# Per-layer input product moved into the last pair of the second attention, gate taken token half by token half, squares of two layer norms summed by VectorE

## The chip, the core and the metric

The kernel runs on one core of a Trainium2 chip. The metric is the device time of one execution in microseconds (us); lower is better. TensorE (PE in the profile, PEld for its weight loads) multiplies, ScalarE (ACT) applies functions and copies, VectorE (DVE) adds and scales, GpSimd (POOL) splits weights, and DMA queues are fed by SyncE (SP) and by ScalarE (ACTq). Each engine runs its own list of instructions in order and waits on semaphores for the others.

## What is computed

A hybrid layer (convolution and windowed attention), then a layer with forgetting attention and a feed-forward net, for 1024 tokens of width 1024 in float32. The change touches the end of it. With `x` the output of the first layer:

```python
o = fox_mixer(x, w_in, b_f, w_out)             # second attention: 16 heads, causal, log forget gates
y = layer_norm(ALPHA * x + o, ln_mix_g, ln_mix_b)
f = conv_ffn(y, w_up, conv_w, conv_b, w_down)
y = layer_norm(ALPHA * y + f, ln_ffn_g, ln_ffn_b)
out = y + sigmoid(y @ ple_w_gate + ple_b_gate) * (p @ ple_w_proj)
```

`p` is the per-layer input, 256 features for each token; `p @ ple_w_proj` depends on nothing else in the kernel.

## The kernel before

Activations stand feature-major: a tile has 128 features on the partitions, `KT` = 8 tiles make the width, and the 1024 tokens are the free axis, cut into two halves of 512 (`HALF`, `hs(h)`). Each float32 operand is kept as a high part and a low part, and a product of a weight block and an operand block is three matmuls (hi by hi, hi by lo, lo by hi) of 512 columns. A *unit* is a 128-column slab of a weight matrix: SyncE loads it in two pieces into `raw`, GpSimd's `split` makes `whi` and `wlo` of it, in one of two slots. Half a product tile (8 k-blocks, 24 matmuls) goes to `bank0` or `bank1`; its eviction raises `tile_out`.

**The second attention** runs head pair by head pair (`forget_pair`, 8 pairs). A pair has 16 steps s: 8 query blocks for each of two heads, with 1 to 8 key blocks. In a step, in program order: TensorE transposes the probabilities (`flip_p(s)`), multiplies the values of the step before at even s (`values(s - 1)`), and makes `scores(s + 3)`. ScalarE does `normalise(s + 1)`, the fold of the pair of heads at s = 4, 8, 12 (`fold`), copies the transposed block out (`high(s)`, which at even s also waits for `values(s - 1)`), and does `expo(s + 2)`. VectorE does maximum (`maxima(s + 2)`), low part (`low`) and reciprocal (`inverse(s + 2)`). Between the steps of a pair TensorE computes the input product of the following pair. The last pair has none to compute after its first eight blocks. The attention's output is split by `forget_hi` (ScalarE, 128x1024 into `a_lo`) and `forget_lo` (VectorE, into `a_hi`): tiles 0 to 3 in steps 0, 1, 2 and 9 of the last pair, tiles 4 to 7 behind it.

**The output product** (`out_half`) goes through all tiles for token half 0, then for half 1. VectorE evicts each with two operations, ALPHA times the high and ALPHA times the low part of x, and adds it to `acc` for the mean. During half 1 the layer norm n1 of half 0 runs: TensorE multiplies `acc` by a matrix of 1/1024 (`mean`), VectorE subtracts (`centre`), ScalarE squares (`square`), TensorE sums the squares over features (`squares`, one float32 product for each tile), ScalarE takes ln and exp (`root`), and VectorE and ScalarE scale and split (`scaled_and_lo`, `norm_hi`). `half_pass(0)` of the feed-forward net waits for these.

**The end.** The down products of half 1 (`down_half`) run with the norm n2 of half 0 among them. Behind them stand the eight `ple_tile`s (p times its weight: 16 halves of 12 matmuls), with the mean and the eight `squares` of half 1 between, and then `gate_half` for 8 units and 2 halves; each unit of the gate is split once. Sigmoid, product, sum and store follow tile by tile.

Order is written out by hand in each engine's list; nothing is scheduled automatically.

Of the kernel before, what the change touches and what calls it, by code (L numbers as in the profile page):

```python
# [166 lines left out]

LEAVES = {s + 1: PARTS[s][-1] // 8 for s in range(NST) if PARTS[s][-1] % 8 == 7}
# [5 lines left out]
def build(nc, xT, weights, pair_weights, cols, pT, out, y_scr, ga_scr, t_scr, g_scr, c_scr, h_scr):  # L174
    ctx = ExitStack()
    with ctx:
# [52 lines left out]
        def psum(name, n):  # L229
# [45 lines left out]
            ("f_fold", [P, HALF], F32), ("f_raw", [P, S], F32), ("fk_lo0", [P, S], F32R))  # L275
        f_klo = ((fk_lo0, fk_lo1_even), (fk_lo0, fk_lo1_odd))
# [56 lines left out]
        p_hi = ((slot_hi[12], slot_lo[12]), (slot_hi[21], slot_lo[21]))  # L333
        ple = [slot_f[2 * m:2 * m + 2] for m in range(KT)]
        g_sig, g_out = slot_f[16:18], slot_f[18:20]
        (p_raw,) = overlay(stage_b_at, ("p_raw", [P, PLE_KT, S], F32))
        (p_lo,) = overlay(stage_b_at, ("p_lo", [P, PLE_KT, S], F32R))

# [22 lines left out]
        mg_in = [sem(f"mg_in{s}") for s in range(2)]  # L361
# [6 lines left out]
        c_in = [sem(f"c_in{h}") for h in range(2)]  # L368
        z_part = sem("z_part")
        zeros_made = sem("zeros_made")  # L370
# [24 lines left out]
        cols_made = sem("cols_made")  # L395
        p_in = sem("p_in")
        ple_hi = sem("ple_hi")
        ple_lo = sem("ple_lo")
# [84 lines left out]
        def _(pool):  # L483
# [121 lines left out]
        def _(pe):  # L605
# [172 lines left out]
            def forget_pair(it, pp, fills):  # L778
# [1860 lines left out]
```

## Time and profile before

| | us |
|---|---|
| median of 3 runs (lowest, highest) | 2717.56 (2715.29, 2719.19) |
| the profiled execution | 2716.53 |
| its span in the trace | 2714.6 |
| TensorE busy | 2611.3 (96%) |
| VectorE, ScalarE, GpSimd busy | 1405.0, 1061.5, 1276.3 |

All stretches below are from this one execution, in us from the start of its span. The last pair of the second attention lies at about 1690 to 1766, the output product behind it up to about 1873, the last down product ends at about 2585.6, and the last gate matmul is issued at 2708.97. The clock of TensorE is given as a share of full speed: 1.00 is 2.4 GHz, 0.50 is 1.2 GHz.

### The profile page before, as it was taken

The page shows a single profiled execution, that of the slowest core. Times are in us where ns is not written, and L with a number is a line of the kernel's source. Part 1 is how long each engine was busy: PE and PEld are TensorE (multiplying, and loading weights), DVE is VectorE, ACT ScalarE, POOL GpSimd, SP SyncE. Part 2 cuts the span into 40 slices and gives each one's busy share as a digit, 9 for nine tenths or more (in the row PEclk, how much of TensorE's full clock was granted, in tenths as well). Part 3 has the DMA queues.
Part 4 walks back from the last instruction along what each step waited for, and adds up shares of the span by engine and source line. Part 5 has one row for each costly group of instructions (what it writes and reads, how often), then busy time and mean ns, then how long its engine had stood idle before and what let it go on. Part 6 is the DMA issues. An engine that isn't in the chain of part 4 may idle for free.

```text
span 2714.6 us, 37373 instructions
## 1 busy us (share of the span) xinstructions
PE 2611.3 (96%) x12136; PEld 2103.9 (78%) x12136; DVE 1405.0 (52%) x2033; ACT 1061.5 (39%) x1932; POOL 1276.3 (47%) x1060
## 2 busy tenths in 40 slices
PE   8999999999999989999999999799999999999999
PEld 5788888877777778888888888576778888787777
DVE  5455542035555655435555555556865655613443
ACT  4333321065455531127677766603333333301231
POOL 3788873332222214431111111075688787576733
PEclk9999999999999999999999999799999999999999
DMA  2222225310111114221111111021222222633312
GB/s 102 83 77 67 64 98 177 108 39 32 45 40 39 39 70 140 95 78 38 46 40 39 39 39 40 8 86 62 90 85 81 81 82 71 207 97 124 102 56 83
DMA packets 94718, 202.99 MB, mean 75 GB/s; under 512 B 10384, under 2 KB 10512, under 8 KB 94624
## 3 DMA queue, kind: packets, MB, share of 16 engines
q1 hardware_dynamic: 69824, 127.43, 14.9%
q10 hardware_dynamic: 24800, 74.36, 7.7%
q8 instruction: 52, 0.85, 0.1%
q14 instruction: 42, 0.34, 0.0%
HBM read 169.18 MB, written 32.57 MB: 74 GB/s over the span
## 4 chain that ended last, share of the span: by engine, by line
PE 78%; DVE 9%; ACT 7%; issue 4%; POOL 1%; DMA 1%; ACTq 0%; DVEq 0%; POOLq 0%
PE bank L611 18%; PE bank L669 17%; PE bank L872 13%; PE flip L872 6%; PE flip L1032 4%; PE pv L1032 4%; PE bank L1078 3%; PE pv L872 3%; PE pv L822 2%; PE score L631 1%; DVE z L1884 1%; PE flip L807 1%; PE score L794 1%; PE bank L807 1%; PE score L791 1%
## 5 line engine op out<-in xcount | busy, mean ns | idle before, releaser
L516 POOL TENSOR_SCALAR whi<-raw 128x512 fp32r<-128x512 f32 x334 | 252.9, 757 | 1277.1 <-PE bank L669 724.2
L518 POOL TENSOR_TENSOR wlo<-raw,whi 128x512 fp32r<-128x512 f32 x334 | 478.9, 1434 | 27.8
L611 PE MATMUL bank<-a_hi,whi 128*128 128x512 f32 x464 | 185.4, 400 | 3.5 <-POOL wlo L518 2.0
L611 PE MATMUL bank<-a_lo,whi 128*128 128x512 f32 x464 | 186.2, 401 | 0.5 <-DVE a_hi L2030 0.5
L669 PE MATMUL bank<-b_hi,whi 128*128 128x512 f32 x384 | 154.9, 403 | 5.6 <-DVE fk_lo_odd L2024 3.2
L611 PE MATMUL bank<-b_hi,whi 128*128 128x512 f32 x368 | 148.4, 403 | 9.8 <-DVE b_lo L1894 7.7
L531 POOL TENSOR_TENSOR wlo<-a,whi 128x512 fp32r<-128x512 f32 x102 | 148.5, 1455 | 14.5 <-ACT whi L1401 14.5
L669 PE MATMUL bank<-a_hi,whi 128*128 128x512 f32 x368 | 148.9, 405 | 6.2 <-DVE s_z L1971 5.1
L669 PE MATMUL bank<-b_hi,wlo 128*128 128x512 f32 x384 | 151.7, 395 | 0.0
L669 PE MATMUL bank<-b_lo,whi 128*128 128x512 f32 x384 | 151.3, 394 | 0.0
L611 PE MATMUL bank<-b_lo,whi 128*128 128x512 f32 x368 | 146.7, 399 | 2.3 <-DVE b_hi L1926 2.3
L669 PE MATMUL bank<-a_hi,wlo 128*128 128x512 f32 x368 | 145.5, 395 | 0.0
L669 PE MATMUL bank<-a_lo,whi 128*128 128x512 f32 x368 | 145.4, 395 | 0.0
L611 PE MATMUL bank<-a_hi,wlo 128*128 128x512 f32 x336 | 132.6, 395 | 0.0
L1401 ACT ACTIVATE whi<-a 128x512 fp32r<-128x512 f32 x102 | 63.4, 628 | 123.5 <-PE bank L872 51.5
L1299 ACT ACTIVATE fp<-fp,neg_max 128x128 f32<-128x128 f32 (+7 forms) x128 | 99.2, 775 | 26.9 <-DVE neg_max L2050 26.3
L1305 ACT ACTIVATE fp<-fp,row_inv 128x128 f32<-128x128 f32 (+7 forms) x128 | 99.4, 776 | 25.7 <-DVE row_inv L2055 24.9
L611 PEld LDWEIGHTS bank<-a_hi,whi 128*128 128x128 f32 x464 | 87.7, 189 | 26.2 <-issue 4.4
L611 PEld LDWEIGHTS bank<-a_lo,whi 128*128 128x128 f32 x464 | 87.7, 189 | 25.3 <-issue 2.8
L2046 DVE CUSTOM_DVE_ANT_0 fp<-score,fc 128x128 f32<-128x128 f32 (+7 forms) x128 | 96.6, 755 | 15.2 <-issue 5.4
L611 PE MATMUL bank<-b_hi,wlo 128*128 128x512 f32 x240 | 95.6, 398 | 0.0
L611 PEld LDWEIGHTS bank<-b_hi,whi 128*128 128x128 f32 x368 | 70.0, 190 | 30.2 <-DVE b_lo L1894 10.2
(526 smaller groups left out, 7285.8 us busy)
## 6 DMA issues: line engine op xcount, KB each, us to landing
raw<-in_w SPq DMA_DIRECT2D x334, 256.0 KB, 2.6
a<-in_pairs SPq DMA_DIRECT2D x136, 256.0 KB, 2.6
h_scr<-up_y ACTq DMA_DIRECT2D x22, 512.0 KB, 2.6
fc<-c_scr ACTq DMA_DIRECT2D x16, 512.0 KB, 3.6
stage<-h_scr ACTq DMA_DIRECT2D x22, 256.0 KB, 3.4
a<-h_scr ACTq DMA_DIRECT2D x21, 256.0 KB, 3.6
y_scr<-up_y ACTq DMA_DIRECT2D x8, 512.0 KB, 2.7
t_scr<-y_room ACTq DMA_DIRECT2D x8, 512.0 KB, 3.0
```

The lines of the kernel that those rows point to most:

```text
L516: nc.gpsimd.tensor_scalar(hi, src, 1.0, 1.0, ALU.mult, ALU.mult).then_inc(w_hi, 1)
L518: nc.gpsimd.tensor_tensor(lo, src, hi.bitcast(F32), ALU.subtract).then_inc(w_lo, 1)
L531: nc.gpsimd.tensor_tensor(ring[1][pos], src[:].rearrange("p (k c) -> p k c", c=P), ring[0][pos].bitcast(F32), ALU.subtract).then_inc(ww_lo, 1)
L611: last = nc.tensor.matmul(psum_ap, ws[w][:, k, :], a[:, kt, hs(h)], start=(first and i == 0 and j == 0), stop=(final and i == n - 1 and j ...
L669: last = nc.tensor.matmul(bank[b][:], ws[slot][:, k, :], a[:, k, hs(h)], start=(k == 0 and j == 0), stop=(k == KT - 1 and j == 2))
L872: last = nc.tensor.matmul(dst[:], ring[w][pos][:, k, :], a, start=(k == 0 and j == 0), stop=(k == KH - 1 and j == 2))
L1032: last = nc.tensor.matmul(down_bank[m % 2][:], w[ws][:, wk, :], a, start=(k == 0 and j == 0), stop=(k == FT - 1 and j == 2))
L1078: last = nc.tensor.matmul(bank[h][:], w[u % 2][:, k, :], a, start=(k == 0 and i == 0), stop=(k == KT - 1 and i == 2))
L1299: nc.scalar.activation(fp[s % 3][:, 0:w], fp[s % 3][:, 0:w], ACT.Exp, bias=neg_max[:, one], accum_out=row_sum[:, one]).then_inc(fx.exp, 1)
L1305: nc.scalar.activation(fp[s % 3][:, 0:w], fp[s % 3][:, 0:w], ACT.Copy, scale=row_inv[:, s % 4:s % 4 + 1]).then_inc(fx.prob, 1)
L1401: nc.scalar.activation(ring[0][pos], src[:].rearrange("p (k c) -> p k c", c=P), ACT.Copy).then_inc(ww_hi, 1)
L2046: v.tensor_tensor_reduce(out=fp[s % 3][:, 0:w], in0=score[s % 2][:, 0:w], in1=fc[hh][:, 0:w], scale=SCALE, scalar=-3.0e38, op0=ALU.subtrac ...
```

## The change

- `ple_tile` goes away from the end. In the last pair `ple_part(i)` computes half h = i % 2 of output tile m = i // 2 (6 to a half where `p` is kept whole: 2 k-blocks by 3 matmuls), always in `bank[0]`, at the end of the step that `PLE_LATE` names (part s - 2 in steps 2 to 11), two of them early (`PLE_EARLY`). Even parts are evicted by ScalarE, odd ones by VectorE, at the end of the step that `PLE_OUT` names (part s - 3 in steps 3 to 11), into the last tile of `b_lo`; ScalarE issues a store of each to a scratch tensor `ple_scr`. A part starts when the part before it has been evicted.
- For that room GpSimd first adds the halves of x: `b_hi_f = b_hi + b_lo`, 8 operations of 128x1024 (`x_whole`). The attention output's high part goes to `b_lo` instead of `a_lo`, for tiles 0 to 6 in steps 1 to 7, tile 7 behind the pair. `p` is loaded by two DMAs on ScalarE's queue and split in steps 0 and 1.
- The eviction of the output product loses its second operation (low part of x).
- For n1 of half 0 and n2 of both halves the squares are added by VectorE (`square_add`, 7 of them), and TensorE does one product on the sum (`square_sum`).
- The gate goes through all 8 units for half 0, then again for half 1: 16 units are loaded and split. `mean(n2, 1)` stands behind the first, `square_sum(n2, 1)` behind the second.
- The stored parts are loaded again by 16 DMAs of 256 KB on ScalarE's queue. Product, sum and store of the output are made in place there, one half tile at a time.

```diff
+PLE_EARLY = {12: (10,), 15: (14,)}
+PLE_OUT = {s: (s - 3,) if s < 12 else (9, 10) if s == 12 else (s - 2,) for s in range(3, NST)}
+PLE_LATE = {s: s - 2 if s < 12 else s - 1 if s < 15 else s for s in range(2, NST)}
...
+            for j in range(KT):
+                nc.gpsimd.tensor_tensor(b_hi_f[:, j, :], b_hi[:, j, :].bitcast(F32), b_lo[:, j, :].bitcast(F32), ALU.add).then_inc(x_whole, 1)
...
+            def square_sum(ns, h, adds):
+
+                pe.wait_ge(ns.summed, adds)
+                nc.tensor.matmul(score[1][:, hs(h)], feat_mean[:], acc[:, hs(h)], start=True, stop=True).then_inc(ns.sq_used, KT)
...
+            def ple_part(i):
+
+                m, h = divmod(i, 2)
+                u = U_PLE + m // 4
+                if i == 0:
+                    pe.wait_ge(conv_lo, KT + PLE_KT)
+                if h == 0:
+                    pe.wait_ge(w_lo, u * 2 + 2)
+                    pe.wait_ge(tile_out[0], T_PLE + m)
+                    pe.wait_ge(tile_out[1], T_PLE + m)
+                else:
+                    pe.wait_ge(tile_out[0], T_PLE + m + 1)
+                for k in range(PLE_KT):
+                    for j, (ws, a) in enumerate(((whi, p_hi[k]), (whi, p_lo[k]), (wlo, p_hi[k]))):
+                        last = nc.tensor.matmul(bank[0][:], ws[u % 2][:, 2 * (m % 4) + k, :], a[:, hs(h)],
+                                                start=(k == 0 and j == 0), stop=(k == PLE_KT - 1 and j == 2))
+                last.then_inc(tile_done[h], 1)
...
                     flip_p(s)
                     if s and s % 2 == 0:
                         values(s - 1)
+                    if not fills:
+                        for i in PLE_EARLY.get(s, ()):
+                            ple_part(i)
                     if s + 3 < NST:
                         scores(s + 3)
+                    if not fills and s in PLE_LATE:
+                        ple_part(PLE_LATE[s])
...
-                elif j <= 4:
-                    squares(n1, 0, (2 * j - 2, 2 * j - 1))
+                elif j == 4:
+                    square_sum(n1, 0, KT - 1)
...
+            gate_half(0)
+            mean(n2, 1)
+            gate_half(1)
+            square_sum(n2, 1, 2 * (KT - 1))
+            for i in range(2, 2 * KT):
+                gate_half(i)
...
+            def square_to_sum(ns, h, j):
+
+                act.wait_ge(ns.centred, h * KT + j + 1)
+                if j >= 3:
+                    act.wait_ge(ns.summed, h * (KT - 1) + (j - 2))
+                dst = sq[j % 2][:] if j else acc[:, hs(h)]
+                nc.scalar.activation(dst, z[:, j, hs(h)], ACT.Square).then_inc(ns.sq, 1)
...
             def forget_hi(j):
 
-                act.wait_ge(fx.o, 4 * (NPAIR - 1 if j < 4 else NPAIR))
-                nc.scalar.activation(a_lo[:, j, :], f_o[:, j, :], ACT.Copy).then_inc(fx.o_hi, 1)
+                act.wait_ge(fx.o, 4 * (NPAIR - 1 if j < KT - 1 else NPAIR))
+                act.wait_ge(x_whole, j + 1)
+                if j == KT - 1:
+                    for h in range(2):
+                        act.wait_ge(ple_stored[h], 16 * KT)
+                nc.scalar.activation(b_lo[:, j, :], f_o[:, j, :], ACT.Copy).then_inc(fx.o_hi, 1)
...
+            def ple_out(i):
+
+                m, h = divmod(i, 2)
+                room = b_lo_f[:, KT - 1, hs(h)]
+                if h == 0:
+                    if m:
+                        act.wait_ge(ple_stored[0], 16 * m)
+                    else:
+                        act.wait_ge(x_whole, KT)
+                    act.wait_ge(tile_done[0], T_PLE + m + 1)
+                    nc.scalar.activation(room, bank[0][:], ACT.Copy).then_inc(tile_out[0], 1)
+                act.wait_ge(tile_out[h], T_PLE + m + 1)
+                act.dma_start(ple_scr[m, :, hs(h)], room).then_inc(ple_stored[h], 16)
...
             for j in range(KT):
                 out_half(j, j // 2, j % 2, 1, KT + j)
+                for k in range(max(2 * j - 2, 1), min(2 * j, KT)):
+                    square_add(n1, 0, k)
...
             for j in range(KT):
                 centre(n2, 1, j)
-            scaled_and_lo(n2, 1, None, None, C_LN2G, C_LN2B, range(KT))
+            for j in range(1, KT):
+                square_add(n2, 1, j)
```

TensorE, last pair, around step 4 (`flip`, `bank`: transposed probabilities; `pv`: values; `score`: scores). Before:

```order
L807 MATMUL flip<-ident,fp_121 128x128 x3
L807 MATMUL bank<-ident,fp_121 128x128 [waits fx_lo]
L822 MATMUL pv<-fp_hi,fv 128x256 [waits fx_lo]
...
L791 MATMUL score<-fk_114,fq_113 128x512 [waits fx_max]
L794 MATMUL score<-fk_lo_129,fq_113 128x512
L791 MATMUL score<-fk_114,fq_113 128x512
L793 MATMUL score<-mask_r,ident_r 128x128
L794 MATMUL score<-fk_lo_129,fq_113 128x512
L807 MATMUL flip<-ident,fp_122 128x128 [waits fx_lo,fx_prob]
```

In the changed kernel (`fq_even`, `fk_even`, `p_lo` hold the parts of p here):

```order
L820 MATMUL score<-fk_114,fq_113 128x512
L822 MATMUL score<-mask_r,ident_r 128x128
L823 MATMUL score<-fk_lo_129,fq_113 128x512
L803 MATMUL bank<-fq_even,whi_52 128x512 [waits tile_out1,tile_out0,w_lo]
L803 MATMUL bank<-p_lo_131,whi_52 128x512
L803 MATMUL bank<-fq_even,wlo_54 128x512
L803 MATMUL bank<-fk_even,whi_52 128x512
L803 MATMUL bank<-p_lo_132,whi_52 128x512
L803 MATMUL bank<-fk_even,wlo_54 128x512
L836 MATMUL flip<-ident,fp_122 128x128 [waits fx_lo,fx_prob]
```

A part of six matmuls, with its wait on both `tile_out`, now stands between the scores and the transposes of the next step.

ScalarE, last pair, steps 3 and 4. Before:

```order
L1313 ACTIVATE fp_hi<-bank 128x4x128 [waits fx_flipped]
L1299 ACTIVATE fp_122,row_sum<-fp_122,neg_max 128x768 [waits fx_neg_max]
L1305 ACTIVATE fp_122<-fp_122,row_inv 128x768 [waits fx_inv]
L1320 ACTIVATE f_fold<-pv 64x512 [waits fx_pv,fx_o]
L1313 ACTIVATE fp_hi<-flip 128x4x128 [waits fx_flipped,fx_pv]
L1313 ACTIVATE fp_hi<-bank 128x128 [waits fx_flipped,fx_pv]
L1299 ACTIVATE fp_120,row_sum<-fp_120,neg_max 128x896 [waits fx_neg_max]
```

In the changed kernel (with the numbers of the tiles that are told apart):

```order
L1362 ACTIVATE fp_hi_123<-bank1 128x4x128 [waits fx_flipped]
L1348 ACTIVATE fp2_122,row_sum_68<-fp2_122,neg_max_67 128x768 [waits fx_neg_max]
L1316 ACTIVATE b_lo_74<-f_o_118 128x1024 [waits x_whole,fx_o]
L1336 ACTIVATE b_lo_f_196<-bank0 128x512 [waits tile_done0,x_whole]
L1338 DMA ple_scr<-b_lo_f_196 128x512 [waits tile_out0]
L1354 ACTIVATE fp2_122<-fp2_122,row_inv_70 128x768 [waits fx_inv]
L1369 ACTIVATE f_fold_127<-pv 64x512 [waits fx_pv,fx_o]
L1362 ACTIVATE fp_hi_123<-flip 128x4x128 [waits fx_flipped,fx_pv]
L1362 ACTIVATE fp_hi_123<-bank1 128x128 [waits fx_flipped,fx_pv]
L1348 ACTIVATE fp0_120,row_sum_68<-fp0_120,neg_max_67 128x896 [waits fx_neg_max]
L1316 ACTIVATE b_lo_74<-f_o_118 128x1024 [waits x_whole,fx_o]
L1338 DMA ple_scr<-b_lo_f_196 128x512 [waits tile_out1]
```

A copy of an attention output tile, an eviction and a store's issue have come between the exponential of one step and the normalisation of the next.

ScalarE at the end, half 1 of n2, in the changed kernel (before, the eight squares stood there with evictions of `ple` tiles, and no sigmoid until behind the norm):

```order
L1127 ACTIVATE sq0_76<-z_75 128x512 [waits n2_centred]
L1127 ACTIVATE sq1_77<-z_75 128x512 [waits n2_summed,n2_centred]
L1127 ACTIVATE sq0_76<-z_75 128x512 [waits n2_summed,n2_centred]
L1910 ACT_TABLE_LOAD
L1910 ACTIVATE b_hi_f_195<-bank0,cst_60 128x512 [waits tile_done0]
L1127 ACTIVATE sq1_77<-z_75 128x512 [waits n2_summed,n2_centred]
L1127 ACTIVATE sq0_76<-z_75 128x512 [waits n2_summed,n2_centred]
L1127 ACTIVATE sq1_77<-z_75 128x512 [waits n2_summed,n2_centred]
```

From the fourth square on each waits for an addition of VectorE, whose additions stand behind all eight of its subtractions.

## Rows read from the trace of the kernel before

**Rows 1.** Page, parts 1 and 4: busy time of the engines; chain that ended last.

```profile
PE 2611.3 (96%) x12136; PEld 2103.9 (78%) x12136; DVE 1405.0 (52%) x2033; ACT 1061.5 (39%) x1932; POOL 1276.3 (47%) x1060
...
PE 78%; DVE 9%; ACT 7%; issue 4%; POOL 1%; DMA 1%; ACTq 0%; DVEq 0%; POOLq 0%
```

**Rows 2.** Busy time by stretch; last numbers: granted clock, DMA share, GB/s.

```profile
1626.00:1693.00 67.00, 64.35 (x372) 54.18 (x371) 39.11 (x104) 47.16 (x95) 11.38 (x12) 1.00 0.12 40
...
1701.00:1765.00 64.00, 45.74 (x216) 37.48 (x217) 37.87 (x87) 41.31 (x75) 0.00 (x0) 0.79 0.02 5
```

**Rows 3.** Timeline of ScalarE, last pair: start, duration, engine, line, operation, idle before.

```profile
1711.67 0.94 ACT L1299 ACTIVATE fp<-fp,neg_max 128x768 f32<-128x768 f32 x1 [1.16 <-DVE neg_max L2050]
...
1738.68 0.92 ACT L1299 ACTIVATE fp<-fp,neg_max 128x768 f32<-128x768 f32 x1
...
1751.00 0.48 ACT L1313 ACTIVATE fp_hi<-bank 128x384 fp32r<-128x384 f32 x1
```

**Rows 4.** Groups by line and shape, 1550 to 1760: busy, mean ns of one, idle before.

```profile
L1313 ACT ACTIVATE fp_hi<-flip 128x512 fp32r<-128x512 f32 x26 | 15.4, 592 | 9.9 <-PE pv L822 5.1 <-PE flip L807 4.5
...
L1299 ACT ACTIVATE fp<-fp,neg_max 128x896 f32<-128x896 f32 x6 | 6.3, 1044 | 0.0
...
L1289 ACT ACTIVATE a_lo<-f_o 128x1024 fp32r<-128x1024 f32 x5 | 5.2, 1045 | 0.8 <-DVE f_o L2067 0.8
L2030 DVE TENSOR_TENSOR a_hi<-f_o,a_lo 128x1024 fp32r<-128x1024 f32 x4 | 4.9, 1226 | 3.1 <-ACT a_lo L1289 3.1
```

**Rows 5.** Timeline of GpSimd, the last split before the last pair's steps.

```profile
1699.13 1.29 POOL L518 TENSOR_TENSOR wlo<-raw,whi 128x512 fp32r<-128x512 f32 x1
```

**Rows 6.** Timeline of TensorE: product of p at the end, and two matmuls at 1758.

```profile
2585.69 0.39 PE L1057 MATMUL bank<-t2hi,whi 128*128 128x512 f32 x1
...
2588.24 0.40 PE L1057 MATMUL bank<-t4lo,wlo 128*128 128x512 f32 x1
...
1758.20 0.63 PE L611 MATMUL bank<-a_lo,whi 128*128 128x512 f32 x1
1758.62 0.63 PE L611 MATMUL bank<-a_hi,whi 128*128 128x512 f32 x1
```

**Rows 7.** Timeline of ScalarE and its queue, the end: eviction, store, table load, last sigmoid.

```profile
2588.68 0.60 ACT L1845 ACTIVATE b_lo_f<-bank 128x512 f32<-128x512 f32 x1 [0.80 <-PE bank L1057]
...
2620.34 1.28 ACT L1864 ACT_TABLE_LOAD   x1
...
2709.46 0.69 ACT L1864 ACTIVATE b_lo_f<-bank,cst 128x512 f32<-128x512 f32 x1 [4.89 <-PE bank L1078]
...
2712.23 0.34 ACTq L1867 DMA_DIRECT2D out_y<-f2lo  x1
```

**Rows 8.** Timeline of VectorE: step from the last pair to the output product, and n1.

```profile
1760.93 4.63 DVE L2030 TENSOR_TENSOR a_hi<-f_o,a_lo 128x1024 fp32r<-128x1024 f32 x4 [1.13 <-ACT a_lo L1289]
...
1767.59 0.69 DVE L2351 SCALAR_TENSOR_TENSOR z<-b_lo,z  x1
1768.32 1.67 DVE L2355 TENSOR_TENSOR acc<-acc,z 128x512 f32<-128x512 f32 x1
...
1856.97 1.77 DVE L2351 SCALAR_TENSOR_TENSOR z<-b_lo,z 128x512 f32<-128x512 f32 x1
...
1867.48 1.62 DVE L1894 SCALAR_TENSOR_TENSOR b_lo<-z,cst,b_hi 128x512 fp32r<-128x512 f32 x2
```

**Rows 9.** Timeline of TensorE: squares of n1, and the end from the mean on.

```profile
1839.59 1.88 PE L631 MATMUL score<-sq,feat_mean 128*128 128x512 f32 x4
...
2588.48 1.02 PE L624 MATMUL score<-acc,feat_mean 128*128 128x512 f32 x2
2588.93 0.79 PE L1057 MATMUL bank<-t2hi,whi 128*128 128x512 f32 x1
...
2708.97 0.40 PE L1078 MATMUL bank<-b_hi,wlo 128*128 128x512 f32 x1
```

**Rows 10.** Timeline of VectorE, the end: subtractions of half 1.

```profile
2589.53 4.87 DVE L1879 TENSOR_TENSOR z<-z,score 128x512 f32<-128x512 f32 x8 [2.24 <-PE score L624]
```

More of the change, by code:

```diff
@@ L166 @@
 PARTS = [range(sum(FILL[:s]), sum(FILL[:s + 1])) for s in range(NST)]
+PLE_EARLY = {12: (10,), 15: (14,)}
+PLE_OUT = {s: (s - 3,) if s < 12 else (9, 10) if s == 12 else (s - 2,) for s in range(3, NST)}
+PLE_LATE = {s: s - 2 if s < 12 else s - 1 if s < 15 else s for s in range(2, NST)}
+assert sorted([*PLE_LATE.values(), *(i for x in PLE_EARLY.values() for i in x)]) == list(range(2 * KT))
 LEAVES = {s + 1: PARTS[s][-1] // 8 for s in range(NST) if PARTS[s][-1] % 8 == 7}
@@ L332, in build @@
         y_at = (13, 22)
[L333 to L337, printed above, removed]
+        ple = [[slot_f[24], slot_f[25], slot_f[42], slot_f[43], *(x[:] for x in stage[5:])], slot_f[0:8]]
+        g_sig = slot_f[16:18]
         def sem(name):
@@ L360, in build @@
         row_in = [sem(f"row_in{s}") for s in range(2)]
-        mg_in = [sem(f"mg_in{s}") for s in range(2)]
+        side_in = [sem(f"side_in{s}") for s in range(2)]
         m_sum = sem("m_sum")
@@ L970, in out_half @@
                 pe.wait_ge(tile_out[c], j + (T_FOUT + h * KT // 2))
-                product(bank[c][:], (U_FOUT + c) % 2, a_lo, a_hi, range(KT), range(KT), h).then_inc(tile_done[c], 1)
-            half(U_FOUT, T_FOUT, U_FOUT % 2, a_lo, a_hi, 0, fx.o_lo)
+                product(bank[c][:], (U_FOUT + c) % 2, b_lo, a_hi, range(KT), range(KT), h).then_inc(tile_done[c], 1)
+            half(U_FOUT, T_FOUT, U_FOUT % 2, b_lo, a_hi, 0, fx.o_lo)
             out_half(0, 1, 1, 0)
@@ L1339, in forget_pair @@
                         expo(s + 2)
-                    if not fills and s in (0, 1, 2, 9):
-                        forget_hi(min(s, 3))
+                    if not fills:
+                        if s == 0:
+                            p_high(1)
+                        elif s < KT:
+                            forget_hi(s - 1)
+                        for i in PLE_OUT.get(s, ()):
+                            ple_out(i)
                     if fills and s == NST - 1:
@@ L1346, in forget_pair @@
                         sums_in(*following, s // 15)
+                if not fills:
+                    ple_out(2 * KT - 2)
+                    ple_out(2 * KT - 1)
                 fold(NST - 1)
@@ L1664, in _ @@
                 forget_pair(NPAIR // 2 - 1, pp, pp == 0)
-            for j in range(4, NPAIR):
-                forget_hi(j)
+            forget_hi(KT - 1)
             def evict(i):
@@ L1829, in _ @@
             for j in range(KT):
-                square(n2, 0, j, True)
-            for k in range(PLE_KT):
-                act.dma_start(p_raw[:, k, :], pT[k, :, :]).then_inc(p_in, 16)
+                square_to_sum(n2, 0, j)
             root(n2, 0, eps_ln)
@@ L1868, in _ @@
+            for i in range(5, 2 * KT):
+                gate_out(i)
+                gate_store(i - 1)
+            gate_store(2 * KT - 1)
             act.wait_ge(out_stored, 32 * KT)
@@ L2587, in lay_out @@
     seq += [*down] * 2
[L2588 removed]
+    seq += [*units(a["ple_w_gate_2"][0])] * 2
     weights = np.stack(seq)
```

273 lines of the change are left out of this document (147 added, 126 removed).

## The prediction

> **What bounds the kernel now.** I read the page's first part and its chain first: TensorE is busy for 96% of the span and holds 78% of the chain [rows 1]. So what leaves TensorE's list comes off the time, unless TensorE waits there, and a step put where it waits is free only if nobody waits for that step. Next the busy time by stretch [rows 2]: the seventh pair keeps TensorE busy for 64.35 of 67 us at full clock, but in the last pair, which has no product to fill with, it is busy 45.74 of 64 us and its mean granted clock is 0.79. The change puts work there. The timelines say what bounds that stretch: the loop from transposes to copy to exponential to transposes. Step 3's exponential ends at 1712.6 (1711.67 + 0.94), step 11's at 1739.6, and the last copy of step 14 at 1751.5 [rows 3]: 38.9 us for the eleven steps 4 to 14, 3.5 us each.
>
> **The last pair: start.** Room for the evictions is there when GpSimd has done 8 additions of 128x1024. The trace has none; the nearest is its 128x512 subtraction, 1.29 us [rows 5], so I take 2.5 us each, 20 us from 1700.4: 1720.5. In the same time VectorE has five operations of 1.23 us with two SBUF inputs (two low parts of p, three `forget_lo`) [rows 4]. Such pairs get in each other's way: an addition to `acc` beside GpSimd's split took 1.67 us, its neighbour that reads PSUM 0.69 [rows 8]. With all five in GpSimd's way it is 1726.6. The Trainium skill's GPSIMD Engine Reference (section 8, Key points) says that VectorE instructions with two SBUF inputs contend with GpSimd; the trace agrees (1.67 against 0.69), and without that rule this term would be 3 us smaller.
>
> ScalarE comes to `ple_out(0)` at the end of step 3, near 1718, since it has also waited for the second half of p and copied both (2 x 1.05, like `a_lo` [rows 4]). It waits for all eight additions, then copies (0.60 [rows 7]): 1721 to 1727, taken as 1724.5, where step 3 ended at 1712.6. **+11.9 us** (9 to 15).
>
> **The last pair: steps.** Part s - 2 waits in step s for the eviction of part s - 3, which is the last thing in step s of ScalarE (even) or VectorE (odd). The transposes of step s + 1 stand behind the part on TensorE, and ScalarE's copy behind those. So every step is now one serial chain from eviction to eviction, where before the transposes were done while ScalarE still worked on the step before. Matmuls of p are issued 0.232 us apart (2.55 us over 11 gaps [rows 6]), so a part is 1.4 us.
> Step 9: hand-over 0.1, part 1.4, transposes 0.45, copy 0.25, exponential and its sum 0.75, eviction 0.65 = 3.6. Step 6: hand-over 0.1, part 1.4, transposes 0.9, values 1.4 (which an even step's copy waits for), hand-over 0.15, copies 0.85, exponential 0.5, then `forget_hi` 0.95, `forget_lo` 1.23 and VectorE's eviction 0.7: 8.2. Copies are 0.59, exponentials up to 1.04 at 896 columns [rows 4]; they overlap by 0.1.
> In this way steps 4 to 7 give 8.6, 5.8, 8.2, 5.4; 8 to 11: 5.9, 3.6, 4.6, 4.4; 12 (two parts) 8.8; 13 and 14: 5.3, 5.4. That is 66.0 against 38.9: **+27.1 us** (22 to 31).
>
> **Its end.** Part 14 waits for part 13's eviction, part 15 for part 14's, and the last values stand behind them; that costs about what the shorter tail gives back. Before, the last four `forget_lo` took 4.63 us from 1760.93 [rows 8], and three of them now lie in the pair (-3.4), but `forget_hi(7)` waits for the last store. I count **+0.3**.
>
> **Its clock.** The chain holds 30 us of TensorE's work in steps 4 to 14 (12 parts, 17 us; transposes 6.6; values 7). Matmuls of 512 columns are 0.23 us apart at 2.4 GHz and 0.42 at 1.2 GHz [rows 6], and before the clock was low for part of this stretch, behind idle of 1 to 2 us [rows 2]. The new chain leaves TensorE idle for 2 to 4 us at the end of steps 4 to 7. Bounds are 0 (always fast) and, with half the work slow, 16; I take **+9**.
>
> The pair: 11.9 + 27.1 + 0.3 + 9 = **+48.3 us** (35 to 62).
>
> **Output product, n1 of half 0.** One square is two records, 0.86 us net (four records 1.88 with overlap [rows 9]); seven of them leave TensorE: 6.0 us. But VectorE now does two additions in each period beside an `acc` addition of 1.67, with GpSimd splitting; these cost 1.1 to 1.7 each, so it falls behind, and `square_sum` behind the fifth half waits 5 to 7 us. That gives the 6.0 back. What stays is the removed second eviction (0.69 to 1.77 each [rows 8]) in the stretch up to 1869, where `half_pass(0)` waits for VectorE: three of them, 3.5 us less about 1: **-2.5** (-4 to 0).
>
> **n2 of half 0.** Seven squares less among the down products, where TensorE never waits: 6.0; `square_sum` stands 12 half units behind the mean, 33 us, so the additions are done. The low part of p no longer delays VectorE's eviction at 2554: 0.8 more. **-6.8** (-7.5 to -5).
>
> **The end.** Before: from the last down product at 2585.6 to TensorE's end at 2709.4 (last issue 2708.97 [rows 9]) are 123.8 us: 22.3 for p, 7.7 for squares and mean, 91.4 for the gate, the rest short waits. After: gate half 0 (24 matmuls, 5.6), mean 0.9, gate half 1: 12.2. Then `square_sum` waits. VectorE's eight subtractions take 4.87 and begin 1.05 behind the mean's start [rows 9, 10]: they end at 11.6 behind the down product. Only then comes the first addition, and from the fourth on ScalarE's squares (0.63) wait for additions with two buffers in turn; between them stands a table load of 1.28 and a sigmoid of 0.69 [rows 7]. Addition by addition that ends at 18.8 (17 to 20.5): TensorE idles 6.6 us. Then the sum 0.9, 14 gate halves of 5.58 (78.1), 1.5 for a slow start behind the idle and 1 for GpSimd: its split took up to 5.0 of each 5.6 us in the output product, where each half also had its own unit. 100.3 in all: **-23.5** (-27 to -20).
> Behind TensorE's end one sum instead of two: **-0.6**. The 32 new DMAs are hidden: loads at the end have over 8 us before VectorE asks.
>
> **Sum.** 48.3 - 2.5 - 6.8 - 23.5 - 0.6 = +14.9: 2716.5 becomes 2731.4. That execution lies 1.0 under the median 2717.56, so I forecast 2732.5.
>
> **Rivals.**
> *TensorE's idle takes the parts up (faster).* If the chain is looser than I count, the pair pays only what TensorE lacks: 16 x 1.4 = 22.3 us of parts against 64 - 45.74 = 18.3 us idle, +4, and 9 for the room: +13. Against 33.4 at the other places: 2697. For it: ScalarE is busy for only 41.31 of 64 us [rows 2]. Against: the order of TensorE's list, part before transposes, and the wait on both evictions. It decides from +33 on: below that the change gains. 0.22.
> *Every step starts slow (much slower).* Clock +16, room +15, steps +31, the rest as above: 2717.5 + 62 - 33 = 2747. For it: 0.42 us spacing at 1758, behind idle [rows 6]; against: parts make TensorE busier. 0.12. The Trainium skill's TensorE: Matmul & The Clock Gate (Part 1) says that the default is throttled and activity releases it; by that alone each step behind an idle end would begin at 1.2 GHz, which is this rival. That the mean was 0.79 and not 0.5 speaks for a mixture.
> *Light ends, even (no change).* Clock +2, room +9, steps +24, against 33: 2719. 0.15.
> *The idle at the end is not there.* If additions keep pace with squares, the end gives 30 instead of 23.5, and the forecast falls to 2726; that is inside my case.
>
> **How the numbers follow.** My case has 0.51, with its own range of 2723 to 2742. Within 0.2% (5.4 us, about what can be told from no change here) lie the third rival and a few hundredths of mine: 0.17. Faster: the first rival and the tail of mine: 0.25. Slower: 0.58. For 8 in 10 the range takes in most of the first rival and of the second: 2698 to 2748.
>
> **What would show it.** In the trace of after: the last pair from its first step to the output product some 48 us longer; ScalarE's first eviction there waiting for GpSimd until 1721 or later; transposes that wait for evictions or come behind parts, in steps of 4 to 8 us; low clock in steps 4 to 7. At the end TensorE idle for about 6 us ahead of the sum over squares, its last matmul about 100 us behind the last down product. In n1 a wait of 5 to 7 us behind the fifth half. I am wrong if the step stays near 4 us, if GpSimd's additions are much under 2.5 us, or if the clock stays at 1.00 in the pair.

## The result and the profile after

The changed kernel takes 2741.28 us (median; 2739.40 to 2745.55), the kernel before 2718.06 beside it: a ratio of 1.0089, 95% interval 1.0072 to 1.0107. It is slower, by 23.2 us where 15 were forecast, and inside the range. The profiled execution took 2741.9 us with a span of 2740.1.

I cut both traces at four rows: VectorE's first copy of the values of the last pair, its first eviction of the output product, the last matmul of the down product and TensorE's last matmul. These are the four in the changed kernel (timelines of VectorE and TensorE: start, duration):

```profile
1694.52 0.69 DVE L1986 TENSOR_TENSOR fv<-flip,fv 128x512 fp32r<-128x512 f32 x1 [3.30 <-ACT fv L1159]
...
1814.63 0.69 DVE L2448 SCALAR_TENSOR_TENSOR z<-b_hi_f,bank 128x512 f32 x1 [0.81 <-PE bank L617]
...
2626.69 0.40 PE L1067 MATMUL flip<-t2hi,wlo 128*128 128x512 f32 x1
...
2734.90 0.40 PE L1093 MATMUL bank<-b_hi,wlo 128*128 128x512 f32 x1
```

In the kernel before they start at 1697.41, 1766.78, 2585.45 and 2708.97. The same cut was made in each kernel run below, in us:

| kernel | up to the cut | last pair | output product to down product | end | behind it |
|---|---|---|---|---|---|
| before | 1697.4 | 69.4 | 818.7 | 123.5 | 5.6 |
| before, second profile | 1700.9 | 67.9 | 821.0 | 123.5 | 5.7 |
| changed | 1694.5 | 120.1 | 812.1 | 108.2 | 5.2 |
| forecast for the change | | +48.3 | -9.3 | -23.5 | -0.6 |
| measured | -2.9 | +50.7 | -6.6 | -15.3 | -0.4 |
| e1_slack | 1695.4 | 90.1 | 809.8 | 106.7 | 5.2 |
| e2_room | 1698.4 | 116.3 | 809.4 | 108.0 | 5.2 |
| e3_thin | 1697.5 | 104.4 | 810.7 | 105.1 | 5.2 |
| e4_sums | 1696.4 | 66.8 | 814.0 | 123.6 | 5.7 |
| e6_end | 1694.3 | 121.3 | 809.8 | 102.6 | 5.2 |
| e7_slack_room | 1698.1 | 85.6 | 809.6 | 107.4 | 5.2 |
| e10_shift | 1699.8 | 82.5 | 810.9 | 106.8 | 5.2 |
| e11_all | 1697.9 | 82.7 | 810.8 | 101.4 | 5.3 |
| e12_pe_squares | 1695.9 | 120.1 | 810.4 | 104.6 | 5.2 |
| e13_mixed | 1701.3 | 82.3 | 811.8 | 103.8 | 5.2 |
| e14_adds_alone | 1697.1 | 72.7 | 816.9 | 123.5 | 5.7 |

The five differences add to the span's 25.5 us. The stretch up to the cut, in which nothing is changed, moves by up to 7 us from execution to execution, so stretches are compared, not spans.

**The start of the pair.** First GpSimd's eight additions, then three of VectorE's operations beside them, then ScalarE's first eviction of a part (start, duration, idle before):

```profile
1697.48 23.47 POOL L578 TENSOR_TENSOR b_hi_f<-b_hi,b_lo 128x1024 f32<-128x1024 f32 x8
...
1697.64 3.27 DVE L2113 TENSOR_TENSOR p_lo<-p_raw,fq_even 128x1024 fp32r<-128x1024 f32 x1
...
1704.14 3.39 DVE L2108 TENSOR_TENSOR a_hi<-f_o,b_lo 128x1024 fp32r<-128x1024 f32 x1
...
1710.40 2.76 DVE L2108 TENSOR_TENSOR a_hi<-f_o,b_lo 128x1024 fp32r<-128x1024 f32 x1 [0.78 <-ACT b_lo L1316]
...
1720.98 0.60 ACT L1336 ACTIVATE b_lo_f<-bank 128x512 f32<-128x512 f32 x1 [4.75 <-POOL b_hi_f L578]
```

An addition took 2.93 us (23.47 / 8). The eviction ended 27.1 us behind the first of the four rows (called the cut from here on), where step 3's exponential had ended 15.2 behind it [rows 3]: +11.9.

**One step.** TensorE in step 6, from one part of the p product to the next:

```profile
1739.84 0.50 PE L803 MATMUL bank<-fq_even,whi 128*128 128x512 f32 x1 [2.65 <-ACT b_lo_f L1336]
...
1742.14 1.05 PE L836 MATMUL flip<-ident,fp 128*128 128x128 f32 x4
...
1745.29 0.33 PE L823 MATMUL score<-fk_lo_odd,fq_odd 128*128 128x256 f32 x1
1749.62 0.47 PE L803 MATMUL bank<-fq_even,whi 128*128 128x512 f32 x1 [4.00 <-DVE b_lo_f L2124]
```

The part waits for ScalarE's eviction, the transposes (L836) stand behind the part, and then TensorE does nothing for 4.00 us until VectorE's eviction. In the whole pair these waits are (us in total, times, longest):

```profile
PE bank L803 <- ACT b_lo_f L1336: 20.4, 7, 12.1
PE bank L803 <- DVE b_lo_f L2124: 20.3, 7, 4.4
```

and by stretch (busy us and counts of TensorE, its weight loads, VectorE, ScalarE, GpSimd; granted clock, DMA share, GB/s), where [rows 2] had 45.74 of 64 us at 0.79:

```profile
1710.00:1721.60 11.60, 0.00 (x0) 0.00 (x0) 8.20 (x10) 4.13 (x7) 10.95 (x4) 0.63 0.00 1
1721.60:1732.40 10.80, 6.51 (x24) 5.39 (x24) 3.48 (x7) 4.26 (x7) 0.00 (x0) 0.66 0.06 24
1732.40:1739.80 7.40, 4.62 (x15) 3.82 (x15) 2.97 (x8) 4.47 (x7) 0.00 (x0) 0.69 0.09 35
1739.80:1749.40 9.60, 5.79 (x28) 4.98 (x28) 4.09 (x10) 3.45 (x6) 0.00 (x0) 0.82 0.07 27
```

In the last three no engine is busy for two thirds of the time: the order bounds them, not an engine. None of the idle time ahead of an eviction in the pair ended with a store (one ended with GpSimd's addition, 4.75 us, three with a part of TensorE, 10.7 us), so the one room held nobody up beyond its first use.

**The end.** VectorE's subtractions [rows 10] and additions of squares, then TensorE's sum and the start of the seventh gate half (a gate half is one `gate_half`, 24 matmuls):

```profile
2633.62 4.87 DVE L1950 TENSOR_TENSOR z<-z,score 128x512 f32<-128x512 f32 x8 [4.69 <-PE score L630]
2638.41 4.70 DVE L1963 TENSOR_TENSOR acc<-acc,sq 128x512 f32<-128x512 f32 x4
2643.70 3.78 DVE L1963 TENSOR_TENSOR acc<-acc,sq 128x512 f32<-128x512 f32 x3 [0.58 <-ACT sq L1127]
...
2647.62 2.05 PE L643 MATMUL score<-acc,feat_mean 128*128 128x512 f32 x2 [8.44 <-DVE acc L1963]
...
2676.25 0.77 PE L1093 MATMUL bank<-t3hi,whi 128*128 128x512 f32 x1 [3.17 <-POOL wlo L521]
```

TensorE waits 8.44 us for the sum and 3.17 us ahead of the seventh gate half. The row puts the second wait down to a split, but that split is already the following unit's. The seventh half's own ended at 2673.25, and what ended just before TensorE went on is ScalarE's sigmoid of the fifth gate half, which frees the bank:

```profile
2671.65 1.60 POOL L521 TENSOR_TENSOR wlo<-raw,whi 128x512 fp32r<-128x512 f32 x1
...
2674.85 0.72 ACT L1150 ACTIVATE b_hi<-z,cst 128x512 fp32r<-128x512 f32 x1 [1.99 <-DVE z L1955]
...
2675.48 0.67 ACT L1910 ACTIVATE b_hi_f<-bank,cst 128x512 f32<-128x512 f32 x1
```

The sigmoid ended at 2676.15, 0.1 us before TensorE's row. The fifth half had been ready since 2667; in ScalarE's list its sigmoid stands behind the last high part of the norm (L1150), which waited for VectorE's scaling (L1955). Behind each of the two waits TensorE's clock is low:

```profile
2648.00:2652.00 4.00, 4.00 (x9) 2.43 (x9) 2.19 (x4) 2.64 (x3) 0.00 (x0) 0.54 0.37 131
2652.00:2656.00 4.00, 4.00 (x19) 3.25 (x18) 2.58 (x4) 2.64 (x4) 0.00 (x0) 1.00 0.00 0
...
2676.00:2680.00 4.00, 3.75 (x9) 3.02 (x10) 3.96 (x5) 0.73 (x2) 2.29 (x2) 0.50 0.35 122
2680.00:2684.00 4.00, 4.00 (x14) 3.14 (x13) 1.33 (x2) 0.00 (x0) 0.00 (x0) 0.70 0.35 124
```

### The profile page after: what moved, and what is told of

It is laid out like the page before. It is cut to its first block, busy times and chain, and to the rows that moved or that the text cites. A ratio compares the mean times of both kernels' runs of the same rounds, so it can differ in the third digit from the quotient of the medians.

```text
span 2740.1 us, 37493 instructions
## 1 busy us (share of the span) xinstructions
PE 2602.0 (95%) x12094; PEld 2103.9 (77%) x12094; DVE 1425.3 (52%) x2044; ACT 1058.6 (39%) x1923; POOL 1322.0 (48%) x1100
## 4 chain that ended last, share of the span: by engine, by line
PE 76%; DVE 8%; ACT 6%; issue 4%; POOL 3%; DMA 2%; ACTq 0%; DVEq 0%; POOLq 0%; SPq 0%
PE bank L617 19%; PE bank L680 17%; PE bank L906 13%; PE flip L906 6%; PE pv L906 3%; PE pv L1067 3%; PE flip L1067 3%; PE bank L1093 3%; PE pv L851 2%; DMA raw<-in_w 1%; PE bank L803 1%; PE flip L836 1%; POOL wlo L521 1%; PE score L823 1%; POOL b_hi_f L578 1%
## 5 line engine op out<-in xcount | busy, mean ns | idle before, releaser
L521 POOL TENSOR_TENSOR wlo<-raw,whi 128x512 fp32r<-128x512 f32 x350 | 503.5, 1439 | 29.2
L617 PE MATMUL bank<-b_lo,whi 128*128 128x512 f32 x496 | 199.0, 401 | 2.3 <-DVE b_hi L2004 2.3
L680 PE MATMUL bank<-b_lo,whi 128*128 128x512 f32 x384 | 151.3, 394 | 0.0
L680 PE MATMUL bank<-a_lo,whi 128*128 128x512 f32 x368 | 145.4, 395 | 0.0
L617 PE MATMUL bank<-a_lo,whi 128*128 128x512 f32 x336 | 132.6, 395 | 0.0
L617 PEld LDWEIGHTS bank<-b_lo,whi 128*128 128x128 f32 x496 | 94.3, 190 | 26.9 <-DVE b_hi L2004 4.0
L1463 ACT ACTIVATE whi<-a 128x512 fp32r<-128x512 f32 x102 | 63.5, 628 | 123.5 <-PE bank L906 51.5
L617 PE MATMUL bank<-b_lo,wlo 128*128 128x512 f32 x256 | 101.3, 396 | 0.0
```

What stands on the lines that cost most here:

```text
L521: nc.gpsimd.tensor_tensor(lo, src, hi.bitcast(F32), ALU.subtract).then_inc(w_lo, 1)
L617: last = nc.tensor.matmul(psum_ap, ws[w][:, k, :], a[:, kt, hs(h)], start=(first and i == 0 and j == 0), stop=(final and i == n - 1 and j ...
L680: last = nc.tensor.matmul(bank[b][:], ws[slot][:, k, :], a[:, k, hs(h)], start=(k == 0 and j == 0), stop=(k == KT - 1 and j == 2))
L1463: nc.scalar.activation(ring[0][pos], src[:].rearrange("p (k c) -> p k c", c=P), ACT.Copy).then_inc(ww_hi, 1)
```

## Experiments

In e1_slack and e3_thin theory 1 is the prediction's: the pair is one serial chain, through the one bank of the parts. Its rivals were that the work, the load of the engines or only GpSimd's additions set the steps.

**Evictions one step earlier (e1_slack).** In the changed kernel step s evicts part s - 3 while TensorE does part s - 2.

```diff
-PLE_OUT = {s: (s - 3,) if s < 12 else (9, 10) if s == 12 else (s - 2,) for s in range(3, NST)}
+PLE_OUT = {3: (0, 1), 12: (10, 11), **{s: (s - 2,) for s in range(4, 12)}, **{s: (s - 1,) for s in range(13, NST)}}
```

> The changed kernel, but each part of the p product is evicted one step earlier (at the end of the step in which its matmuls are issued), so that the next part finds its bank free. Theory 1 (the chain eviction, part, transposes, copy sets the steps): steps 4 to 14, 76.5 us from the third to the fourteenth step's last eviction in the changed kernel, fall by 15 to 25 us, TensorE's waits for evictions ahead of parts (40.7 us in sum) mostly go, and the time is 2717 to 2727 against 2741.3. Theory 2 (TensorE's work at a low clock and the load of ScalarE and VectorE set the steps): less than 5 us comes back, 2736 or more.

Measured: 2711.16 us, ratio to the kernel before 0.9976 (0.9967 to 0.9985). The pair falls from 120.1 to 90.1 us, and the time is under the 2717 to 2727 of theory 1: the chain cost more than that theory asked for. Waits and three stretches:

```profile
PE bank L803 <- ACT b_lo_f L1336: 15.2, 5, 12.1
PE bank L803 <- DVE b_lo_f L2123: 1.1, 2, 0.8
...
1722.00:1730.00 8.00, 7.50 (x30) 6.31 (x31) 3.29 (x7) 3.42 (x6) 0.00 (x0) 0.67 0.18 67
1730.00:1740.00 10.00, 7.22 (x45) 5.72 (x43) 6.04 (x14) 7.33 (x13) 0.00 (x0) 1.00 0.14 52
1740.00:1750.00 10.00, 8.48 (x50) 6.96 (x50) 7.88 (x19) 7.28 (x17) 0.00 (x0) 1.00 0.14 55
```

Of the waits, 40.7 us, only 16.3 are left, and 12.1 of these are the first one. The work is the same, all 16 parts; evicting most of them one step earlier carries 30 us, 24.4 of them in these waits. The clock, which I had priced by itself, came back with the waits: 1.00 from 1730 on. The Trainium skill's TensorE: Matmul & The Clock Gate (Part 1) says that activity releases the throttled clock; the traces agree (0.66 to 0.82 in the three busy stretches of the changed kernel above, 1.00 here).

**The room at the first addition (e2_room).** GpSimd makes tile 7, whose low part's place is the room, first.

```diff
-            for j in range(KT):
+            for j in (KT - 1, *range(KT - 1)):
                 nc.gpsimd.tensor_tensor(b_hi_f[:, j, :], ...
...
-                        act.wait_ge(x_whole, KT)
+                        act.wait_ge(x_whole, 1)
```

> The changed kernel, but GpSimd makes tile 7 of x first, and the first eviction waits for that tile alone, not for all eight. Theory 1 (the wait for eight additions holds ScalarE for about 12 us): the first eviction comes by 1712 instead of 1721.6, and the time falls by 7 to 11 us, to 2730 to 2734. Theory 2 (VectorE, slowed by GpSimd's additions, would hold the steps just as long): under 3 us.

Measured: 2737.83 us, 1.0072 (1.0056 to 1.0087); the pair is 3.8 us shorter. The gain of 3.5 us lies between the theories: the wait is gone, but the eviction, 26.5 us behind the cut in the changed kernel, still starts 21.6 us behind it (its cut is at 1698.35):

```profile
1719.02 1.04 ACT L1316 ACTIVATE b_lo<-f_o 128x1024 fp32r<-128x1024 f32 x1
1719.96 0.57 ACT L1336 ACTIVATE b_lo_f<-bank 128x512 f32<-128x512 f32 x1
```

So the wait accounts for at most 4.9 of the +11.9 us. The rest lies ahead of it, in steps 0 to 3 themselves, where theory 2 looked for it.

**GpSimd's additions alone (e14_adds_alone).** The kernel before, with the eight additions at their new place and nothing that waits for them but the output product.

```diff
             split(U_FOUT + 1, (U_FOUT + 1) % 2, tile_done[1], U_FOUT)
+            for j in range(KT):
+                nc.gpsimd.tensor_tensor(b_hi_f[:, j, :], b_hi[:, j, :].bitcast(F32), b_lo[:, j, :].bitcast(F32), ALU.add).then_inc(x_whole, 1)
```

(The output product then adds `b_hi_f` and `b_lo`, so that the residual's low part counts twice.)

> The kernel before, with one part of the change alone: GpSimd makes the whole of x with its eight additions of 128x1024 in the first steps of the last pair; no part of the p product is there and nobody waits for the additions before the output product. Theory 1 (what VectorE loses beside them, about 2 us for each of its three subtractions there, 3.39, 2.76 and 2.49 us against 1.23, delays the maxima and with them every step): the last pair, 69.4 us from the first copy of its values to the first eviction of the output product, becomes 73 to 76 us, the time 2720 to 2724. Theory 2 (VectorE has slack there, and only the wait for the additions costs in the changed kernel): within 1.5 us of the kernel before.

Measured: 2723.75 us, 1.0023 (1.0014 to 1.0033); the pair takes 72.7 us against 69.4 and 67.9. The three subtractions, which took 1.23 us each:

```profile
1701.09 2.40 DVE L2032 TENSOR_TENSOR a_hi<-f_o,a_lo 128x1024 fp32r<-128x1024 f32 x1 [0.78 <-ACT a_lo L1291]
...
1706.12 3.00 DVE L2032 TENSOR_TENSOR a_hi<-f_o,a_lo 128x1024 fp32r<-128x1024 f32 x1 [0.78 <-ACT a_lo L1291]
...
1711.98 2.76 DVE L2032 TENSOR_TENSOR a_hi<-f_o,a_lo 128x1024 fp32r<-128x1024 f32 x1 [0.78 <-ACT a_lo L1291]
```

They lose 4.5 us (8.16 - 3.69), and the pair of this profile loses 3.3 to 4.7: that fits theory 1, with VectorE on the path there, since a maximum stands behind each such subtraction. The medians differ by more, 7.4 us (2716.38 beside it); the profiled execution, 2717.87, is the fastest of ten, and where the others lost the rest isn't shown. The Trainium skill's GPSIMD Engine Reference (section 8, Key points) says that such pairs contend; the trace agrees, with this as the price.

**Both edits, and the subtractions moved away (e7_slack_room, e10_shift).** In e10_shift the operations on the attention's output stand in steps 5 to 11:

```diff
-                        elif s < KT:
-                            forget_hi(s - 1)
+                        elif 4 < s < KT + 4:
+                            forget_hi(s - 5)
```

and `forget_lo` likewise.

> The changed kernel with the edits of e1_slack and e2_room together: evictions one step earlier, and the first of them waiting for one addition of GpSimd only. If the wait of 4.75 us adds to the chain: 3 to 5 us under e1_slack, 2706 to 2708. If the looser chain hides it, or a part in the third step costs as much: the same as e1_slack.

> As e7_slack_room, but the operations on the attention's output (copy by ScalarE, subtraction by VectorE) are done from step 5 to 11 instead of 1 to 7, behind GpSimd's additions. In the changed kernel VectorE's three subtractions beside those additions took 3.39, 2.76 and 2.49 us, 1.23 alone. Theory 1 (contention with GpSimd in the first four steps, not only the wait for it, delays the first eviction): 5 to 8 us under e7_slack_room. Theory 2 (the steps behind take up what these lose): no difference to e7_slack_room.

Measured: e7_slack_room 2706.46 us, 0.9955 (0.9938 to 0.9971), pair 85.6; e10_shift 2702.17 us, 0.9941 (0.9924 to 0.9957), pair 82.5. The wait for the room adds to the chain (4.5 us of pair, 4.7 in the medians). What stood beside the additions shows at the first eviction, which starts 21.6 us behind the cut in e7_slack_room and 14.5 in e10_shift, with both low parts of p (3.27 and 1.55 us) still beside the additions. The edit moves the operations whole, not only their contention: the three subtractions took 8.5 us there in e7_slack_room where they take 3.7 alone, so of the 7.1 us at most 4.8 are contention. The pair gives back 3.1 and the medians 4.3, less than the 5 to 8 expected: the steps behind take up the rest. With four runs of each the two intervals overlap, so that last size is uncertain. The two versions are 0.5 to 0.6% under the kernel before, where e1_slack was 0.2% under it; the last pair with all that the change puts there is now 13 to 15 us longer than before instead of 51.

**One matmul per part (e3_thin).**

```diff
-                for k in range(PLE_KT):
-                    for j, (ws, a) in enumerate(((whi, p_hi[k]), (whi, p_lo[k]), (wlo, p_hi[k]))):
-                        last = nc.tensor.matmul(bank[0][:], ...
+                last = nc.tensor.matmul(bank[0][:], whi[u % 2][:, 2 * (m % 4), :], p_hi[0][:, hs(h)], start=True, stop=True)
```

> The changed kernel, but each of the 16 parts of the p product is one matmul instead of six (five sixths of that product are left out), with every wait and eviction kept. A part falls from 1.4 to 0.3 us. Theory 1 (parts lie in a serial chain in steps 4 to 15): 13 parts in the chain give back 14 us, less what a lower granted clock costs: 2724 to 2731. Theory 2 (parts lie in time that the waits leave anyway, and only the waits cost): under 4 us, 2737 or more.

(The kernel leaves out five sixths of that product.)

Measured: 2724.76 us, 1.0028 (1.0017 to 1.0039), pair 104.4. The 80 matmuls left out are 18.6 us at 0.232 each, and 15.8 come back: the parts' work lies in the chain, not in idle time. The waits stay (19.3 and 18.8 us), and the clock was 0.50 to 0.83 in all seven stretches of 10 us from 1725 to 1795. In e1_slack the work is whole and the chain is loose, and that gains twice as much.

**The squares alone (e4_sums).** The kernel before, with `squares(n1, 0, ...)` and `squares(n2, 0, ...)` replaced as in the change.

```diff
-                elif j <= 4:
-                    squares(n1, 0, (2 * j - 2, 2 * j - 1))
+                elif j == 4:
+                    square_sum(n1, 0, KT - 1)
```

> The kernel before, with one part of the change alone: the squares of half 0 of both layer norms are summed by VectorE, and TensorE multiplies once by the matrix of means. The forecast's terms for this part are -6.8 at the second norm and nothing at the first (7 squares, 6.0 us, against a wait of 5 to 7): about -7 us, ratio 0.9974. The trace of the changed kernel shows -2.8 and -3.0 at the two places, with other edits among them: if that is this part's worth, -4 to -6 us, ratio 0.998. If the additions on VectorE hold TensorE as long as the squares did: 0.

Measured: 2709.81 us, 0.9972 (0.9961 to 0.9982), 7.5 us under the 2717.29 beside it: the forecast's -7, not the -4 to -6 read from the changed kernel. The stretch where the squares stand is 814.0 against 818.7 and 821.0: 4.7 to 7.0 less; the rest of this profile's difference lies in the last pair (66.8) and ahead of it, where nothing was changed. The wait that I had forecast at n1 is there:

```profile
PE score L637 <- DVE acc L1908: 6.9, 1, 6.9
```

In the changed kernel, where VectorE has one eviction less in each period, it is 4.5 us.

**The end in another order (e6_end).** The sum stands behind the fourth gate half, the first sigmoid ahead of the squares, and the loads of the second half of the p product behind them.

```diff
             gate_half(1)
-            square_sum(n2, 1, 2 * (KT - 1))
-            for i in range(2, 2 * KT):
+            gate_half(2)
+            gate_half(3)
+            square_sum(n2, 1, 2 * (KT - 1))
+            for i in range(4, 2 * KT):
```

> The changed kernel, with the end in another order: TensorE multiplies the sum of squares by the matrix of means only behind the fourth gate half, ScalarE does the first sigmoid ahead of the squares and the second behind the sixth square, and the loads of the second half of the p product are issued behind the squares. Theory 1 (TensorE's 8.4 us of idle ahead of that matmul, the low clock behind it and a late weight split, 3.2 us, are what the end lost against its forecast): 8 to 12 us come back, 2730 to 2733 against 2741.3. Theory 2 (GpSimd's splits and VectorE's additions cannot keep pace, and TensorE waits for them instead): under 4 us.

Measured: 2735.20 us, 1.0067 (1.0050 to 1.0084); the end 102.6 instead of 108.2. The 8.4 us of idle ahead of the sum are gone, and as much came back in another form:

```profile
PE bank L1093 <- POOL wlo L521: 6.2, 3, 3.3
PE bank L1093 <- issue: 2.2, 1, 2.2
```

Of these, 2.9 us (1.57 and 1.34) are waits for GpSimd's splits, which wait for weights while the loads that I had moved there run, and take long beside VectorE's work (0.62 and 1.29 us undisturbed):

```profile
2650.02 0.62 POOL L519 TENSOR_SCALAR whi<-raw 128x512 fp32r<-128x512 f32 x1 [3.59 <-DMA raw<-in_w]
...
2656.54 0.99 POOL L519 TENSOR_SCALAR whi<-raw 128x512 fp32r<-128x512 f32 x1
2657.61 1.57 POOL L521 TENSOR_TENSOR wlo<-raw,whi 128x512 fp32r<-128x512 f32 x1
```

The other two, 2.22 us at 2667.30 and 3.32 at 2676.45, end 0.1 us behind a sigmoid of ScalarE, as in the changed kernel. The gain of 6.1 us lies between the two theories.

**All edits (e11_all).** The edits of e10_shift and e6_end together.

> As e10_shift, with the end of e6_end too. If the two places are independent, the time is e10_shift's less what e6_end gains over the changed kernel: about 2692 to 2698, 0.7 to 0.9% under the kernel before.

Measured: 2701.65 us, 0.9943 (0.9927 to 0.9960). Its end is 101.4 against e10_shift's 106.8, but the medians differ by 0.5 us: the expected 2692 to 2698 was missed. The profiled execution is the fastest of e11_all and the slowest of e10_shift. Four runs of each, up to 7.8 us apart in e10_shift, don't settle it.

**Squares on TensorE at the end (e12_pe_squares, e13_mixed).** The first undoes that part alone; the second puts the squares between the groups of matmuls of two gate halves of e10_shift.

```diff
-            square_sum(n2, 1, 2 * (KT - 1))
+            squares(n2, 1, range(KT))
```

> The changed kernel, with one part undone at the end alone: the eight squares of half 1 of the second norm go one by one to TensorE behind the second gate half, as in the kernel before, and VectorE adds none of them. TensorE's squares cost 8 times 0.86 us, 6.9, against 8.4 us of idle and 0.9 for the sum. Theory 1 (behind the idle stand a low clock and a late weight split, slowed by VectorE's additions, which go too): 2731 to 2737 against 2741.3. Theory 2 (only the 6 us of TensorE's work count, as the edit intends): 2740 or more, no gain from undoing it.

> As e10_shift, but at the end the squares of half 1 of the second norm go to TensorE one by one between the groups of three matmuls of the second and third gate half, so that TensorE neither waits for VectorE's sum nor for the squares; the first sigmoid comes ahead of the squares. Expected: e10_shift's end of 106.8 us from the last down product to the last gate product falls to 99 to 102, and the time to 2695 to 2699. If GpSimd's splits are the next bound, as in e6_end: 2700 to 2703.

Measured: 2742.57 us, 1.0103 (1.0086 to 1.0120), and 2701.98 us, 0.9941 (0.9924 to 0.9957). In the profiles the ends are 104.6 and 103.8 us, some 3 us shorter than with VectorE's sum; in the medians there is no gain. In the first TensorE still waits 3.1 us ahead of the seventh gate half, again until 0.1 us behind the sigmoid of the fifth (it ends at 2673.73, TensorE starts at 2673.83); its splits were done 3 us earlier. So VectorE's additions did not cause this wait. e13_mixed lies in the 2700 to 2703 expected for splits as the next bound, but not by them: TensorE waits 0.4 us for splits in all, and its one longer wait at the end, 2.65 us, ends 0.1 us behind a sigmoid. What can be said: at the end summing by VectorE wins nothing measurable over TensorE's squares.

**The kernel before again (e15_before_again).**

> The kernel before, unchanged, for a second profile on this chip: how far the shares of the last pair (69.4 us), of the stretch from there to the last down product (818.7) and of the end (123.5) move from one execution to another. If the granted clock alone varies in the pair: 66 to 70 us there, and 0.5 us or less at the end. If all stretches move by several us, differences of that size between single profiles say nothing.

Measured: 2720.79 us. The end repeats to 0.1 us, the pair moves by 1.5 and the middle stretch by 2.4, so both sentences were half right: differences under 3 us outside the end say nothing in single profiles.

## Why the prediction was right, and where it was not

*The pair's start*, +11.9: measured +11.9. GpSimd's last addition set it, as forecast: the additions started where I had them, and one took 2.93 us, between my 2.5 and the 3.3 of my upper bound. ScalarE came 21.7 us behind the cut where I had 20.6, and waited 4.75 us. What I had not seen is why it came late: I put that down to copying p and counted the contention only as time of GpSimd's. But it holds VectorE's maxima, too: without the wait the eviction still starts 21.6 us behind the cut (e2_room), against 26.5 with it. For the same reason I expected 7 to 11 us of e2_room, and 3.5 came.

*The steps*, +27.1, and *the clock*, +9: from the eviction in step 3 (1721.6) to step 14 (1798.1) are 76.5 us against 38.9, +37.6 where 36.1 were forecast. e1_slack and e3_thin show the mechanism: take the slack or the work and the steps shrink. The mistake in form was to price the clock as a term of its own; it hangs on the chain and went with it. How the 37.6 divide between the two terms no run shows: the mean granted clock was 0.81 over these steps and 0.82 over the same steps before.

*The pair's end*, +0.3: +1.2.

*Output product and down products*, -2.5 and -6.8: the profiled execution shows -6.6 in sum, but the ten kernels with the change in this stretch have 809.4 to 812.1, and the two profiles of before 818.7 and 821.0. That is 6.6 to 11.6 less, and -9.3 lies in it. The shortfall in the one profile is no finding.

*The end*, -23.5: measured -15.3, the one step that failed, 8.2 us. Up to the last subtraction the sum held (11.6 us behind the down product, forecast and measured). Then its terms were mis-sized: the seven additions took 9.0 us instead of 7.2 (idle 8.44, not 6.6, +1.8); where I had 1 us for GpSimd's splits, TensorE waited 3.17 us for ScalarE's sigmoid (+2.2); and the matmuls behind the sum, 87.3 us from 2647.62 on against 0.9 + 78.1 + 1.5 + 1, leave 3.6 more, since the clock fell twice: the third and the seventh gate half took 7.4 and 8.5 us instead of 5.58. These make 7.6 of the 8.2. I had let one wait end before I looked for the next: the sum came late, so the norm and VectorE's scaling began late, and the sigmoid that frees the bank stands behind them. GpSimd stood still, too, while TensorE idled (9.54 us), but its split for the seventh half was done 0.2 us behind TensorE's last matmul ahead of the wait, so hardly any of it is GpSimd's. The same order of rows stands in e1_slack, e2_room, e6_end, e10_shift, e11_all and e12_pe_squares (waits of 2.2 to 3.3 us, each ended 0.1 us behind a sigmoid). It is read from the traces; no run moves the sigmoid alone, so what that would win stays open.

*Behind TensorE's end*: -0.4 for -0.6.

Of the rivals, the first (idle takes the parts up, 2697) needed a looser chain: that kernel is e1_slack and its successors, not this one. The second (every step starts slow, 2747) is nearer to the time than the forecast is (5.7 us against 8.8), but not by its mechanism: it had 62 us in the pair, where 50.7 were measured, and the end at -23.5. The time lies at the upper edge of my case's own 2723 to 2742.

## What to carry to other kernels

Work put into idle time can cost its waits on top of its length (here 24 us of waits against 16 for five sixths of the matmuls): before it is moved there, write down for each step which eviction it waits for and who stands behind it, and evict a part in the step in which it is made, so that its bank is free when the next part comes. An operation with two SBUF inputs should not stand beside GpSimd's large additions where a chain runs through VectorE. When a stage starts late, follow what stands behind it in every engine's list: here a sigmoid that frees a bank stood behind the late norm. And when the profile names one engine for a wait on several, compare the times at which each of them was done.

## What the runs showed of the hardware

VectorE's 128x1024 subtraction of two SBUF tiles took 1.23 us alone and 2.40 to 3.39 us beside GpSimd's 128x1024 additions (one low part of p there took only 1.54), while its maxima, whose first input is in PSUM, kept their time (0.94 us for 128x768 at 1713.08, 0.95 before). GpSimd's additions themselves took 2.70 us each where VectorE had three such operations beside them (21.58 for eight in e14_adds_alone), 2.93 where it had five and 2.59 where it had two (20.73 for eight in e10_shift).

The granted clock in the last pair of the unchanged kernel was 0.85 from 1720 to 1730 in one profile and 0.61 in the other: single stretches of a mixed clock differ that much, while the mean over the pair was 0.80 in both.
